# Finishing the latent tokens of a diffusion step: which engine scales the last rows, which store adds the bias, and in which order the last sums are made

## The reference, cut to what matters

```python
ff = expert_choice_ffn(modulate(x, shift2, scale2), w_router, w_gate_up, w_down)
x = layer_norm(ALPHA * x + gate2 * ff, ln2_g, ln2_b)   # (x - mean) * rsqrt(var + eps) * g + b
```

## Time before, and its profile

| what | value |
|---|---|
| median of three runs | 931.21 us (929.11 to 931.85) |
| profiled execution, its own time | 930.54 us |
| its span | 928.5 us |
| busy share of the span | PE 94%, DVE 83%, ACT 63%, POOL 17% |
| mean granted TensorE clock | 0.978 of full speed |

### The profile page before, as it was taken

The page is one execution under the profiler, slowest core; times in us unless marked ns, Lnnn a source line. Parts: engine busy times, 40 slices in busy tenths (PEclk is TensorE's granted clock), DMA queues, the critical chain, the costliest instruction groups (busy, mean ns, idle before and its releaser), DMA issues.

```text
span 928.5 us, 12427 instructions
## 1 busy us (share of the span) xinstructions
PE 869.7 (94%) x5002; PEld 613.8 (66%) x5002; DVE 775.2 (83%) x824; ACT 583.3 (63%) x606; POOL 159.4 (17%) x109
## 2 busy tenths in 40 slices
PE   6989999698899838999999999999999999999995
PEld 5779977466688625666666666666666666666663
DVE  4579654989789876898998998998898998998877
ACT  2365276757622335777777777777777777777653
POOL 0000300010010042003302312311321320320220
PEclk9999999999999958999999999999999999999998
DMA  9920540450086469999999999999999999999717
GB/s 341 387 89 9 203 182 1 182 183 2 11 326 255 193 282 333 375 416 390 401 404 393 395 404 393 390 412 388 386 415 378 386 412 377 382 409 384 264 14 203
DMA packets 59348, 272.78 MB, mean 294 GB/s; under 512 B 6728, under 2 KB 7036, under 8 KB 42908
## 3 DMA queue, kind: packets, MB, share of 16 engines
q1 hardware_dynamic: 50848, 245.33, 67.1%
q0 software_dynamic: 7536, 24.00, 9.1%
q10 hardware_dynamic: 908, 2.68, 0.8%
HBM read 257.99 MB, written 14.00 MB: 293 GB/s over the span
## 4 chain that ended last, share of the span: by engine, by line
PE 81%; DVE 8%; ACT 5%; DMA 3%; issue 2%; SPq 1%; ACTq 0%; DVEq 0%
PE PS L995 23%; PE PS L996 23%; PE PS L997 23%; PE PS L1210 2%; PE PS L1194 2%; DMA w_qkv<-in_w_in 2%; PE PS L1233 1%; PE PS L1363 1%; PE PS L1350 1%; DMA acc_scratch<-ysc,idx_u 1%; PE PS L1164 1%; PE PS L1286 1%; ACT WX L723 1%; ACT xnT L666 1%; PE PS L1018 1%
## 5 line engine op out<-in xcount | busy, mean ns | idle before, releaser
L1895 DVE TENSOR_TENSOR Wl<-wr,Wh 128x2048 fp32r<-128x2048 f32 x190 | 432.6, 2290 | 52.7 <-ACT Wh L909 52.7
L909 ACT ACTIVATE Wh<-wr 128x2048 fp32r<-128x2048 f32 x192 | 367.4, 1914 | 69.8 <-PE PS L997 69.7
L995 PE MATMUL PS<-Wh,Xh 128*80 128x512 f32 x512 | 203.6, 398 | 1.5 <-DVE Xl L1900 0.8
L997 PE MATMUL PS<-Wl,Xh 128*80 128x512 f32 x512 | 201.9, 394 | 0.0
L996 PE MATMUL PS<-Wh,Xl 128*80 128x512 f32 x512 | 201.9, 394 | 0.0
L561 POOL DMA_INDIRECT acc_scratch<-ysc,idx_u x15 | 81.2, 5411 | 418.6 <-DVE ysc L1926 418.6
L997 PEld LDWEIGHTS PS<-Wl,Xh 128*80 128x80 f32 x512 | 76.2, 149 | 42.6 <-issue 0.9
L995 PEld LDWEIGHTS PS<-Wh,Xh 128*80 128x80 f32 x512 | 76.2, 149 | 42.3 <-issue 2.1
L996 PEld LDWEIGHTS PS<-Wh,Xl 128*80 128x80 f32 x512 | 76.3, 149 | 39.7 <-issue 0.7
L995 PE MATMUL PS<-Wh,HTh 128*80 128x512 f32 x256 | 101.6, 397 | 0.0
L996 PE MATMUL PS<-Wh,HTl 128*80 128x512 f32 x256 | 100.4, 392 | 0.0
(11 more groups left out here) (311 smaller groups left out, 1199.2 us busy)
## 6 DMA issues: line engine op xcount, KB each, us to landing
wr<-in_w_gate_up SPq DMA_DIRECT2D x128, 1024.0 KB, 12.6
wr<-in_w_down SPq DMA_DIRECT2D x64, 1024.0 KB, 11.6
ring<-in_w_mod SPq DMA_DIRECT2D x24, 1024.0 KB, 10.1
ring<-in_w_in SPq DMA_DIRECT2D x4, 1024.0 KB, 11.6
ring<-in_w_out SPq DMA_DIRECT2D x4, 1024.0 KB, 6.5
w_qkv<-in_w_in SPq DMA_DIRECT2D x4, 768.0 KB, 14.0
h_scratch<-h POOLq DMA_DIRECT2D x5, 512.0 KB, 5.4
acc_scratch<-xt POOLq DMA_DIRECT2D x5, 512.0 KB, 5.8
```

Of the source, the lines that this page charges most:

```text
L909: act.activation(Wh[n % NWH][:], wr[s][:], ACT.Copy).then_inc(W_hi, 1)
L995: pe.matmul(out, w[0], x[0], start=first, stop=False)
L997: return pe.matmul(out, w[0], x[1], start=False, stop=last)
L1895: dve.tensor_tensor(Wl[s][:], wr[s][:], Wh[n % NWH][:].bitcast(F32), ALU.subtract).then_inc(W_lo, 1)
```

## The change

`FIN_ADD` goes from 2 to 4. So chunks 2 and 3 of `y_sample` are scaled by ACT and stored by an accumulating DMA from POOL, as chunks 0 and 1 are. POOL writes ln2_b to four chunks of `y_sample` instead of two, at the place of L591. DVE's `finished(2)` and `finished(3)` go, as do SP's two plain stores of `y_sample`; SP stores the context chunk alone. ACT's `scaled(2)` stands behind chunk 3's statistics, and `scaled(3)` behind the square root of chunk 4. On PE the order of the sums changes: chunk 1 gets the last expert's rows before it waits for its reload, and chunks 2 to 4 take, half by half, the expert's rows and then the reload. Chunk 0 is as before.

```diff
-FIN_BANK, FIN_ACT, FIN_ADD = (4, 2, 6, 0, 4), 3, 2
+FIN_BANK, FIN_ACT, FIN_ADD = (4, 2, 6, 0, 4), 3, 4
@@ ScalarE
         act.activation(fin[:, 0, 0:1], fin[:, 1, 0:1], ACT.Sqrt, bias=epsc[:, 0:1], scale=1.0 / D).then_inc(std3_ok, 1)
+        scaled(2)
         std3(4, 4)
+        scaled(FIN_ACT)
@@ TensorE
         for c in range(CH):
-            pe.wait_ge(acc_in[c], 16)
             if c == PC:
                 pe.wait_ge(z_ok, 1)
             out = [bank(FIN_BANK[c] + h) for h in range(2)]
-            for h in range(2):
-                pe.matmul(out[h], ident, xf[:, c, 512 * h:512 * h + 512], start=True, stop=False)
+
+            def reloaded(h, first):
+                return pe.matmul(out[h], ident, xf[:, c, 512 * h:512 * h + 512], start=first, stop=not first)
+
+            def scattered_last(h, first):
+                pe.wait_ge(yl_ok, 2 + h)
+                pe.matmul(out[h], hot[1][:, c * P:(c + 1) * P], yh[1][:, 512 * h:512 * h + 512], start=first, stop=False)
+                return pe.matmul(out[h], hot[1][:, c * P:(c + 1) * P], yl[1][:, 512 * h:512 * h + 512],
+                                 start=False, stop=not first)
...
+            elif c == 1:
+                for h in range(2):
+                    scattered_last(h, True)
+                pe.wait_ge(acc_in[c], 16)
+                for h in range(2):
+                    reloaded(h, False).then_inc(fin_ps, 1)
+            else:
+                pe.wait_ge(acc_in[c], 16)
+                for h in range(2):
+                    scattered_last(h, True)
+                    reloaded(h, False).then_inc(fin_ps, 1)
@@ VectorE
-        for c in range(FIN_ADD):
+        for c in range(FIN_ACT):
             fin_stats(c, c + 1)
             centred(c)
             inverse(c).then_inc(z_ok, 1)
-        fin_stats(2, 3)
-        centred(2)
-        finished(2)
-        centred(3)
-        fin_stats(4, 4)
-        finished(3)
-        centred(4)
-        finished(4)
+        centred(FIN_ACT)
+        fin_stats(PC, PC)
+        inverse(FIN_ACT).then_inc(z_ok, 1)
+        centred(PC)
+        finished(PC)
```

More of the change, by code:

```diff
@@ L1415, in _ @@
             out = [bank(FIN_BANK[c] + h) for h in range(2)]
-            for h in range(2):
-                pe.matmul(out[h], ident, xf[:, c, 512 * h:512 * h + 512], start=True, stop=False)
+            def reloaded(h, first):
[5 more added lines that the diff above has]
+                                 start=False, stop=not first)
             if c == 0:
+                pe.wait_ge(acc_in[c], 16)
+                for h in range(2):
+                    reloaded(h, True)
                 pe.wait_ge(yl_ok, 1)
@@ L1422, in _ @@
                     pe.matmul(out[h], hot[0][:], yl[0][:, 512 * h:512 * h + 512], start=False, stop=False)
[L1423 to L1427, removed]
+                for h in range(2):
+                    scattered_last(h, False).then_inc(fin_ps, 1)
+            elif c == 1:
+                for h in range(2):
+                    scattered_last(h, True)
+                pe.wait_ge(acc_in[c], 16)
+                for h in range(2):
+                    reloaded(h, False).then_inc(fin_ps, 1)
+            else:
+                pe.wait_ge(acc_in[c], 16)
+                for h in range(2):
+                    scattered_last(h, True)
+                    reloaded(h, False).then_inc(fin_ps, 1)
     @block.vector
```

## The result

The changed kernel takes 942.18 us (median of four runs, 939.88 to 943.64) against 930.82 us: a ratio of 1.0113, with a 95% interval of 1.0101 to 1.0124, or +10.5 us (9.4 to 11.5). The difference of the two medians is 11.4 us, inside that interval; the text goes by the ratio. I had forecast +2.2 us and a range of 931.2 to 934.9 us. The prediction was wrong: right about the direction, and short by 8 us.

What follows compares the result with a forecast made beforehand. PE held 81% of the chain; the new tail was bound by ACT, POOL and two accumulates. Last landing 929.5 against 927.46 (+2.0) plus 0.26 for POOL gave +2.2: 931.21 + 2.2, 933.4 us, range 931.2 to 934.9.

Steps and rivals of the forecast that it cites:

- the closing 1.1 us, and 0.26 for POOL: End of span: 1.1 us follows the last landing, plus 0.26 us because POOL reacts in 0.29 where SP took 0.03.
- All rivals: Tail stores: starts paid, +3.2 us (chance 0.26); pair overlaps, 0 to +1.4 (0.16); accumulate cheap, -2.1 (0.06).
- the top of the range (+3.7): Upper limit of the predicted time, 934.9 us: unshared starts of the accumulates with some late step on top.
- Two signs that I had named: In the profile: right if the chain ends in a DMA of `out_y_sample`; wrong if a context store still ends last.
- The context store 2.1 us earlier: Tail: SP issues it at 922.76 instead of 924.86, 0.8 us from PE's order and 1.3 from the removed `finished(3)`.
- The last POOL store landing near 929.5: Tail: chunk 3's accumulating store lands there, behind the context store, the pair being bound by the DMA engines.
- the sum: Tail DMA: 920.17 + 8.9 for the accumulating pair, plus the context store's 1.3, less a 0.9 us start: 929.5.
- The cheap accumulate: Rival for the tail: accumulates are cheap with no reload near, so the context store sets the end, -2.1 us; chance 0.06.
- The saved start: Tail: the second accumulate, its descriptors already waiting, doesn't pay the 0.9 us start of a transfer.
- the slower rival: Tail: each accumulate pays its start, 0.9 us not saved; last landing 930.4, span +3.2 us; chance 0.26.
- The extra ln2_b stores at 0: Expert stage: two more 0.5 MB POOL writes are hidden by the prefetch; price 0, at most another 0.1 us.
- PE's order at -0.85 us and no wait for a later reload: Tail: chunk 1 is done about 0.85 us earlier on PE, and the reloads of chunks 2 to 4 arrive in time.

Runs made afterwards that it cites:

- e3: The changed kernel with POOL's four y_sample stores plain, leaving out the addition of ln2_b; ratio 1.0042 to the kernel before, +3.9 us.
- e10: The kernel before with four stores of ln2_b in the expert stage instead of two; ratio 1.0005 to the kernel before.
- e5: The kernel before with only the new order of PE's sums; ratio 0.9995 to the kernel before.
- e6: The changed kernel with the old order of PE's sums; ratio 1.0094 to the kernel before.
- e1: The changed kernel with the last wait for the accumulating stores on SP instead of POOL; ratio 1.0057 to the kernel before, +5.3 us.

## Why the prediction was wrong, point by point

- **The step that failed** is the first paragraph's reading of the end: the context store lands at 927.46 "and the span ends at 928.5, 1.1 us behind that. Nothing else is late: POOL's two accumulating stores land at [...] 917.7 and [...] 920.9". I took the 1.1 us for a closing that follows the last landing, whichever that is, and carried it over as "the closing 1.1 us, and 0.26 for POOL". It was POOL's drain, begun at 921.05, that ended at 928.3. POOL's store at 920.9 was not early: it was the last step but one of the critical path. From POOL's last landing to the end it is 7.6 us before and 8.0 after, where I put 1.3. That is 6.7 of the 7.0 us by which the tail was forecast too short. All rivals took over the same closing, so even the top of the range (+3.7) lay far below the result.
- The chain of waits misled here because it ends with the last instruction that counts as work; the drain is in none of its rows, and the view of waits named PE's sequencer for 0.8 us in before. A look at the block's closing line would have shown it.
- Two signs that I had named point the other way from my forecast: the chain ends with DVE's last instruction and not in a DMA of `out_y_sample`, and the context store still lands last, by 0.2 us (931.0 against 930.8). Neither decided the end.
- **The context store 2.1 us earlier**: right, 1.9 us measured, and worthless, as argued. What the argument missed is that already before the change it wasn't this store that set the end.
- **The last POOL store landing near 929.5**: right, 929.7 on the clock of before. The pair of accumulates with the context store took 9.5 us from the first issue to the last landing, as the sum had it (9.3).
- That this came out is partly luck, for the order of the transfers was not the forecast one. I had put the context store whole between the two accumulates, landed before chunk 3's; here is the traffic from 927.0 to 929.4 us (packets, MB, share of the 16 engines):

```profile
q0 software_dynamic: 79, 0.32, 67.8%
q1 hardware_dynamic: 80, 0.33, 36.0%
```

- The two queues ran mixed, 79 packets of the accumulate to 80 of the store, two thirds of the engines' time for the one and one third for the other, and the store took 6.9 us to land. This doesn't look like what the Trainium skill says in "DMA: Bandwidth & Descriptors", section "Queues, rings and completion order" (a whole packet of 9 to 17 descriptors from one queue before the next), by which the store would have landed ahead of chunk 3's. The trace doesn't name the engine of a packet, so it can't settle how one engine takes its turns. The sum came out because both orders put the same work on the engines.
- **The cheap accumulate**: wrong in every run. It took 5.4 to 6.1 us, and 7.5 to 7.9 as the second of two issued 1.5 us apart. The plain POOL stores of e3 took 2.9 to 3.0 us, near the 3.2 us estimated by the formula of the Trainium skill ("DMA: Bandwidth & Descriptors", section "Anatomy of one DMA — SWDGE (gpsimd) path"). What the formula lacks is thus the accumulation.
- **The saved start** of the second accumulate: it landed 3.8 us behind the first with a 1.3 us store mixed in, so the start was saved. So the slower rival, in which it isn't saved, was not the cause of the slowness either.
- **The extra ln2_b stores at 0**: right for the expert stage. They cost 0.16 us in the drain (7.418 against 7.255 in e10).
- **PE's order at -0.85 us and no wait for a later reload**: right. e5 and e6 give 0.7 and 1.0 us, and PE's timeline shows no wait for the reloads of chunks 2 to 4.
- Three small slips of the sum: the closing is 928.5 - 927.46 = 1.04 us and not 1.1 (the total uses 1.04); a pair reaches +2.8 at 9.8 us from 920.17 and not at 9.6; and the 7.0 us "that the pair took" stand in no row, give 6.7, so that the saved start would be 0.8 us and not 0.9.
- 1.2 us of the profiled difference were there before the first changed instruction. Of the measured 10.5 us the tail explains 9.2; the rest is upstream or in the spread of the runs, and no experiment isolates it.

## What to carry to other kernels

Between the last landing and the end of the span there can be work that no chain shows: look at the closing instructions of every engine before calling anything "not late", and ask of each engine when it may begin to close. Here GpSimd needs some 80 ns of closing for every DMA that it ever issued, so its last DMA should come early, its DMAs be few, and waits for its stores stand on another engine (e1 ran some 5 us faster than the changed kernel for that alone). And a slow store late in the kernel is worth less than the cheap arithmetic that it replaces: DVE's two removed instructions saved 1.3 us of the path and put two accumulates of 5.5 and 7.8 us behind it.

## What the runs showed of the hardware that I had not expected

- POOL's DRAIN at the end of a block: 0.0817 us for each of POOL's DMAs (88 to 108 of them, 7.26 to 8.89 us), with nothing in flight. With POOL's DMAs in flight it ends about half of that behind their last landing. The Trainium skill, in "VectorE: DVE Perf Modes", section "The DRAIN you can't avoid", gives closing drains of about 12 ns on all five engines; SP's 7 ns fits. POOL's doesn't, nor does DVE's of 1.3 us, which runs beside DVE's last instruction.
- An accumulating store of 0.52 MB lands 5.4 to 6.1 us after its issue (7.5 to 7.9 as the second of two 1.5 us apart), a plain one from the same engine 2.9 to 3.0.
- A plain store beside an accumulating one shared the engines' time with it one to two, packet for packet (80 to 79), and landed in 6.9 us instead of 2.6.
